# A gated stage that applies its weight and shift behind the spatial product, and a reordered last pair of attention

## The reference

```python
h = rmsnorm_2(x, norm_mix_g[i])
z = jnp.einsum('bsd,dc->bsc', h, w_in[i])
uv = jax.nn.gelu(z[..., :o1])
z_u, z_v = uv[..., :GMLP_WIDTH], uv[..., GMLP_WIDTH:]
...
a = gmlp_spatial_gating(z_u, z_v, gmlp_ln_g[i], gmlp_ln_b[i], gmlp_w_s[i], gmlp_b_s[i])
b = forgetting_attention(q, k, v, f_logit, b_f[i])
y_a = jnp.einsum('bsc,cd->bsd', a, w_branch_a[i])
y_b = jnp.einsum('bsc,cd->bsd', b, w_branch_b[i])
merged = gate_a * y_a + gate_b * y_b
```

```python
def gmlp_spatial_gating(z_u, z_v, ln_g, ln_b, w_s, b_s):
    v = layernorm(z_v, ln_g, ln_b)
    v = v.reshape(B, S // GMLP_BLOCK, GMLP_BLOCK, GMLP_GROUPS, GMLP_GROUP_DIM)
    ...
    w = jnp.where(mask[None], w_s, jnp.zeros_like(w_s))
    mixed = jnp.einsum('gts,bnsgc->bntgc', w, v) + b_s.T[None, None, :, :, None]
    return z_u * mixed.reshape(B, S, GMLP_WIDTH)
```

## Time and profile before

| | us |
|---|---|
| median of 3 runs | 2146.32 |
| lowest and highest of them | 2143.61 to 2148.26 |
| profiled execution | 2146.56 |
| its span, first to last instruction | 2144.5 |
| TensorE busy in it | 2093.4 |
| VectorE busy in it | 1319.3 |
| ScalarE busy in it | 876.8 |
| GpSimd busy in it | 345.2 |

### The profile page before, as it was taken

One profiled execution on the slowest core, in us unless ns is written; L12 is line 12 of the kernel. 1 busy time (PEld: TensorE's weight loads), 2 busy tenths in 40 slices (PEclk: granted clock), 3 DMA queues, 4 the chain that ended last, 5 costly groups with the idle time before them and its releaser, 6 DMA issues.

```text
span 2144.5 us, 28580 instructions
## 1 busy us (share of the span) xinstructions
PE 2093.4 (98%) x9448; PEld 1719.8 (80%) x9448; DVE 1319.3 (62%) x1597; ACT 876.8 (41%) x1257; POOL 345.2 (16%) x254
## 2 busy tenths in 40 slices
PE   7999999999999999999999999989999999999998
PEld 4888888788878878888887788867888888888876
DVE  5877578668744553333357877767333577547767
ACT  5322223377533342222245656653222344334444
POOL 2999998000000200000000000021000000000000
PEclk8999999899999989999999999999999999999999
DMA  8665664322233323233323222232433233333222
GB/s 290 185 186 174 199 189 141 100 69 68 69 89 103 104 71 97 84 100 98 90 80 104 70 69 68 69 74 65 118 96 92 86 98 90 88 106 98 74 83 88
DMA packets 372868, 226.33 MB, mean 106 GB/s; under 512 B 8481, under 2 KB 361922, under 8 KB 372816
## 3 DMA queue, kind: packets, MB, share of 16 engines
q1 hardware_dynamic: 362976, 193.49, 30.9%
q0 software_dynamic: 9840, 32.16, 5.5%
HBM read 223.52 MB, written 2.10 MB: 105 GB/s over the span
## 4 chain that ended last, share of the span: by engine, by line
PE 90%; DVE 5%; ACT 2%; issue 1%; DMA 1%; SPq 1%; POOL 0%; DVEq 0%; ACTq 0%
PE ps L486 28%; PE ps L487 28%; PE ps L488 28%; PE ps L610 1%; PE ps L598 1%; DVE wl L1437 1%; PE ps L599 1%; PE ps L625 1%; PE ps L626 1%; DVE inv L1461 0%; PE ps L830 0%; DMA xtok<-in_x 0%; DMA wada<-in_w_ada 0%; SPq L384 0%; PE ps L601 0%
## 5 line engine op out<-in xcount | busy, mean ns | idle before, releaser
L486 PE MATMUL ps<-uh,wh 128*128 128x512 f32 x1848 | 729.6, 395 | 12.5 <-DVE ul L1489 5.5
L487 PE MATMUL ps<-ul,wh 128*128 128x512 f32 x1848 | 723.8, 392 | 0.0
L488 PE MATMUL ps<-uh,wl 128*128 128x512 f32 x1848 | 723.3, 391 | 0.0
L1437 DVE TENSOR_TENSOR wl<-raw,wh 128x1024 fp32r<-128x1024 f32 x389 | 562.7, 1451 | 205.1 <-ACT wh L963 198.9
L963 ACT ACTIVATE wh<-raw 128x1024 fp32r<-128x1024 f32 x389 | 407.6, 1052 | 190.3 <-PE ps L488 187.7
L486 PEld LDWEIGHTS ps<-uh,wh 128*128 128x128 f32 x1848 | 349.6, 189 | 85.9 <-issue 13.7
L488 PEld LDWEIGHTS ps<-uh,wl 128*128 128x128 f32 x1848 | 349.6, 189 | 73.8
L487 PEld LDWEIGHTS ps<-ul,wh 128*128 128x128 f32 x1848 | 349.7, 189 | 71.6 <-issue 0.5
L486 PE MATMUL ps<-ah,wh 128*128 128x512 f32 x528 | 208.9, 396 | 0.0
L487 PE MATMUL ps<-al,wh 128*128 128x512 f32 x528 | 208.8, 396 | 0.0
L488 PE MATMUL ps<-ah,wl 128*128 128x512 f32 x528 | 208.8, 395 | 0.0
(11 more groups left out here) (318 smaller groups left out, 2389.4 us busy)
## 6 DMA issues: line engine op xcount, KB each, us to landing
raw<-in_ffn_w_gu SPq DMA_DIRECT2D x88, 512.0 KB, 4.5
raw<-in_w_in SPq DMA_DIRECT2D x57, 512.0 KB, 3.8
ada_ring<-in_w_ada POOLq DMA_DIRECT2D x56, 512.0 KB, 4.1
raw<-in_w_up SPq DMA_DIRECT2D x44, 512.0 KB, 3.8
raw<-in_w_mix_in SPq DMA_DIRECT2D x40, 512.0 KB, 3.9
raw<-in_ffn_w_down SPq DMA_DIRECT2D x32, 384.0 KB, 3.2
raw<-in_ffn_w_down SPq DMA_DIRECT2D x32, 320.0 KB, 3.0
wada<-in_w_ada SPq DMA_DIRECT2D x16, 512.0 KB, 9.8
```

The costliest lines, as they stand in the source:

```text
L486: pe.matmul(dst, lh, rh, start=first, stop=False, skip_group_check=True)
L487: pe.matmul(dst, lh, rl, start=False, stop=False, skip_group_check=True)
L488: return pe.matmul(dst, ll, rh, start=False, stop=last, skip_group_check=True)
L1437: dve.tensor_tensor(wl[:, w], raw[:, w], wh[:, w].bitcast(F32), ALU.subtract).then_inc(w_lo, 1)
```

## The change

Weight and shift of the layer normalisation move behind the mixing. Since w_s mixes positions and the weight is per channel, W(v*g + b) is g*(W v) + W b. DVE no longer multiplies by ln_g and adds ln_b per group. TensorE mixes the bare normalised values and makes W b in three more matmuls of 128x128 per group, into bank 6 or 7. DVE adds that to b_s in a 128x128 tile, and its bias instruction becomes a multiply by a column of ln_g and an add. POOL splits ln_b into high and low parts (a cast and a subtraction per group), and loads three tiles per group in place of four; ln_g comes with the vectors loaded at the start.

The order of the last pair changes. TensorE runs `z_in(0)` and `z_in(1)` before the first head's values, `z_in(2)` and the first `turn_w` before the second head's, and group 0 is normalised before the second head's output is summed. Group 0's tiles are loaded and masked during the first pair. In the group loop z m+3 stands behind mix m for every m up to 4. z is drained into a tile of its own, `gz`, not into halves of `tmp`. The first branch chunk waits for its input tile by tile.

```diff
+Z_BANK = (B_O, 0, 1, 0, 1, 0, 1, 0)
@@ TensorE, attention body
                     if last:
+                        if kind == 2:
+                            pe.wait_ge(A_["o_s"], 2 * p + 1)
                         next_first()
...
-                    if last and kind == 1:
+                    if last:
                         next_middle()
+                    if last and kind == 2:
+                        pe.wait_ge(A_["t_lo"], 6 * p + 3)
+                        turn_forget()
+                        pe.wait_ge(G["z"], 3)
                     values(t, A_, p, 0)
@@ TensorE, merge
+                    dense(nb + 2, 0, 2, kt, xa[0], xa[1], ready=ready_a)
...
+                    dense(nb + 3, 0, 3, kt, xb[0], xb[1])
@@ TensorE, gated stage
+            def third_z():
+                z_in(2)
+                pe.wait_ge(A["att2"]["t_lo"], 6 * 8)
+                turn_w(0)
-            attention("att2", t2, 2, 8, 3, lambda: z_in(0), None, lambda: z_in(1))
+            attention("att2", t2, 2, 8, 3, lambda: z_in(0), lambda: z_in(1), third_z)
...
                     mm = mm3(bank(2 + s % 2, b * P, P), gvh[:, v], gvl[:, v], gwh[:, w], gwl[:, w], True, True)
+                pe.wait_ge(G["b_lo"], m + 1)
+                mm = mm3(bank(6 + s % 2, 0, P), gsr[s][:, 3 * P:4 * P], gsr[s][:, P:2 * P], gwh[:, w], gwl[:, w], True, True)
                 mm.then_inc(G["mix"], 1)
-            z_in(2)
-            turn_w(0)
-            z_in(3)
             for m in range(DT):
                 if m + 1 < DT:
                     turn_w(m + 1)
                 mix_group(m // 4, m % 4)
-                if 1 <= m < 5:
+                if m + 3 < DT:
                     z_in(m + 3)
-                elif 5 <= m < 7:
+                elif m < 7:
                     merge_gate("merge2", 0, m - 5)
@@ ACT
+            def z_out(m):
+                done(AT_["zu"] + m, 0)
+                act.activation(tile(gz, m), bank(Z_BANK[m]), ACT.Gelu_apprx_tanh).then_inc(G["z"], 1)
...
             for m in range(DT):
-                act.wait_ge(G["w_tr"], m + 1)
-                act.activation(gwh[:, (m % 2) * P:(m % 2 + 1) * P], bank(4 + m % 2, 0, P), ACT.Copy).then_inc(G["w_hi"], 1)
-                act.wait_ge(G["n3"], m + 1)
-                act.wait_ge(G["mix"], m + 1)
-                act.activation(gvh[:, :], sq[:, 0:S], ACT.Copy).then_inc(G["v_hi"], 1)
+                if m > 0:
+                    weight_hi(m)
+                    group_hi(m)
                 if m + 2 < DT:
                     split(nb + m + 2 + LEAD, 0)
                 act.wait_ge(G["a"], m + 3)
                 act.activation(tile(gah, m), sq[:, S:2 * S], ACT.Copy).then_inc(G["a_hi"], 1)
-                if m + 2 < DT:
-                    z_out(m + 2)
+                if m + 3 < DT:
+                    z_out(m + 3)
@@ DVE, last pair
+                    if last and kind == 2:
+                        stream_slice(p)
+                        split(AT_["zu"] + LEAD, 0)
+                        f_rows(p)
                     o_sum(p, 0)
-                    if kind == 2:
+                    if kind == 2 and not last:
                         f_rows(p)
+                    if last and kind == 2:
+                        layer_stats()
                     turned_lo(p, 1)
...
+                    elif kind == 2:
+                        split(AT_["zu"] + 1 + LEAD, 0)
+                        first_group()
                     o_sum(p, 1)
@@ DVE, group
-                dve.tensor_tensor(v4, v4, ln_g.unsqueeze(1).to_broadcast([P, ST, P]), ALU.mult).then_inc(G["n2"], 1)
-                dve.tensor_tensor(v4, v4, ln_b.unsqueeze(1).to_broadcast([P, ST, P]), ALU.add).then_inc(G["n3"], 1)
...
+                bf = gsm[s][:, 2 * P:3 * P]
+                dve.tensor_tensor(bf, bank(6 + s % 2, 0, P), bf, ALU.add).then_inc(G["bf"], 1)
...
+                dve.scalar_tensor_tensor(ssq[:, :].rearrange("p (b c) -> p b c", b=ST), bank(2 + s % 2).rearrange("p (b c) -> p b c", b=ST),
+                                         cols[:, C_LNG + m:C_LNG + m + 1], bf.unsqueeze(1).to_broadcast([P, ST, P]),
+                                         ALU.mult, ALU.add).then_inc(G["bs"], 1)
@@ POOL
+            def mask_group(m):
+                pool.wait_ge(G[f"ld{m % 4}"], 48 * (m // 4 + 1))
+                pool.tensor_tensor(gsm[m % 4][:, 0:P], gsm[m % 4][:, 0:P], gmask[:, :], ALU.mult).then_inc(G["mask"], 1)
+                hi = gsr[m % 4][:, 3 * P:4 * P]
+                pool.tensor_copy(hi, gsm[m % 4][:, P:2 * P]).then_inc(G["b_hi"], 1)
+                pool.wait_ge(G["b_hi"], m + 1)
+                pool.tensor_tensor(gsr[m % 4][:, P:2 * P], gsm[m % 4][:, P:2 * P], hi.bitcast(F32), ALU.subtract).then_inc(G["b_lo"], 1)
```

More of the change, by code:

```diff
@@ L215, in build @@
         ncum = place("ncum", [64, S], F32R, late)
-        gah = place("gah", [P, DT * S], F32R, rows(14))
-        gal = place("gal", [P, DT * S], F32R, rows(22))
+        gah = place("gah", [P, DT * S], F32R, rows(22))
+        gal = place("gal", [P, DT * S], F32R, rows(14))
+        gz = place("gz", [P, DT * S], F32, rows(14))
         gvh = place("gvh", [P, S], F32R, rows(8))
@@ L221, in build @@
         gwl = place("gwl", [P, 2 * P], F32R, rows(10) + 1024)
-        gsm = [place(f"gsm{x}", [P, 4 * P], F32, at) for x, at in enumerate((rows(11), rows(12), late, late + row))]
+        gsm_at = (late + row, rows(11), rows(12), late)
+        gsm = [place(f"gsm{x}", [P, 4 * P], F32, at) for x, at in enumerate(gsm_at)]
+        gsr = [place(f"gsr{x}", [P, 4 * P], F32R, at) for x, at in enumerate(gsm_at)]
         ptok = place("ptok", [P, ST * 256], F32, rows(0))
@@ L656, in first_scores, with turn_forget @@
                         turn_values()
+                def turn_forget():
+                    for j in range(ST):
+                        mm = pe.transpose(bank(B_FT, j * P, P), tmp[:, j * P:(j + 1) * P], ident[:, :])
+                    mm.then_inc(A_["f_tr"], 1)
                 def body(p, last, first=False):
@@ L1179, in body @@
                     if last and kind == 2:
[L1180 to L1181 removed]
+                        for b in range(ST):
+                            gelu_rows(b)
+                        split(AT_["zu"] + LEAD, 0)
+                        z_out(1)
+                        act.wait_ge(A_["f_tok"], 1 + pairs)
+                        v = vtok[:, :].rearrange("p (b n) -> p b n", b=ST)[:, :, (pairs - 1) * P:pairs * P]
+                        act.activation(v, v, ACT.Gelu_apprx_tanh).then_inc(G["vg"], 1)
                     if kind == 1:
@@ L1590, in ffn, with normal_group, weight_lo, group_lo @@
                                     scaled_lo(2 * i + r, *lift)
+            def normal_group(m):
+                dve.wait_ge(G["v_lo"], m + 1)
+                for b in range(ST):
+                    x = dve.tensor_scalar(sq[:, b * P:(b + 1) * P], vtok[:, b * D + m * P:b * D + (m + 1) * P], bnmv[:, 2 * b:2 * b + 1],
+                                          rstd[:, b:b + 1], ALU.subtract, ALU.mult)
+                x.then_inc(G["n1"], 1)
+            def weight_lo(m):
+                dve.wait_ge(G["w_hi"], m + 1)
+                w = slice((m % 2) * P, (m % 2 + 1) * P)
+                dve.tensor_tensor(gwl[:, w], bank(4 + m % 2, 0, P), gwh[:, w].bitcast(F32), ALU.subtract).then_inc(G["w_lo"], 1)
+            def group_lo(m):
+                dve.wait_ge(G["v_hi"], m + 1)
+                dve.tensor_tensor(gvl[:, :], sq[:, 0:S], gvh[:, :].bitcast(F32), ALU.subtract).then_inc(G["v_lo"], 1)
+            def first_group():
+                dve.wait_ge(G["sd"], 1)
+                dve.reciprocal(rstd[:, :], rstd[:, :]).then_inc(G["sd"], 1)
+                dve.wait_ge(G["sd"], 2)
+                normal_group(0)
+                weight_lo(0)
+                group_lo(0)
             def attention(name, t, kind, pairs):
@@ L2052, in group @@
-            def group(m):
-                i, s = m // 4, m % 4
-                dve.wait_ge(G["w_hi"], m + 1)
-                w = slice((s % 2) * P, (s % 2 + 1) * P)
-                dve.tensor_tensor(gwl[:, w], bank(4 + s % 2, 0, P), gwh[:, w].bitcast(F32), ALU.subtract).then_inc(G["w_lo"], 1)
-                dve.wait_ge(G["v_hi"], m + 1)
-                dve.tensor_tensor(gvl[:, :], v_, gvh[:, :].bitcast(F32), ALU.subtract).then_inc(G["v_lo"], 1)
+            nb = AT_["zu"]
+            def group(m):
+                s = m % 4
+                if m > 0:
+                    weight_lo(m)
+                    group_lo(m)
```

135 lines of the change are left out of this document (61 added, 74 removed).

## The result

The changed kernel takes 2159.01 us (median; 2157.83 to 2160.46), against 2146.36 for the kernel before: 1.0059 times as long, interval 1.0043 to 1.0075. It is slower, as forecast, but by 12.7 us where 7.0 were forecast, and 1.0 us above the range's end.

What follows compares the result with a forecast made beforehand. TensorE was taken to bound the kernel, with its matmuls, idles and half-clock stretches. Terms -8.0, +6.0, +0.5 and +8.5 of clock gave +7.0 on 2146.56, so 2153.3 us for a median; range 2145 to 2158.

Steps and rivals of the forecast that it cites:

- The mechanism: Mix 1 to mix 5: ACT's drain waits for z m+3, holding gwh and gvh, so TensorE stalls; 11.25 us in all.
- The term: TensorE's wait after each z chunk for drain, gwh, gvh and gvl: 2.25 us, for mix 1 to mix 5.
- The last pair: First z chunk to mix 0: the ACT and DVE chain sets mix 0, 28.2 us after z 0, -8.0 us.
- the clock's term: Low TensorE clock after six new idles: five of six at 1.7 us, +8.5; bounds none and 13.8.
- Rival 1: Low clock after all six new idles at the dearer price: +12.3 us, 2158.6 us; chance 0.13.
- The rest of the sum: Mix 0 to branch a without clock: periods, last mix, bias matmuls and five stalls, 63.5 us, +6.0.
- The branches: First two branch chunks: 11.31 us before, +0.5 as ACT and DVE come late to the second's weight chunk.
- The two idles that were to go: Mix 0 to branch a: idle of 4.42 goes as turn_w 2 follows z 3, 2.90 as the branch waits tile-wise.
- Rival 3: Group loop: ACT reaches gvh in time, so stalls and most clock loss vanish; -12.75 us, 2133.6 us; chance 0.12.
- Rival 4: POOL's 16 new instructions each lengthen a DVE instruction on the chain by 0.22 us: 3.5 us more, 2156.8; chance 0.05.
- The saving on DVE: Multiply and add dropped for 8 groups, some 11 us busy time, costed at nothing since DVE waits for ACT.

Runs made afterwards that it cites:

- The moved drain: Changed kernel with ACT's drain of z m+2 right behind gvh of m, replacing z m+3's drain ahead of gwh: 2137.6 us, 0.9962 times the kernel before.
- the fill: Changed kernel with 11 matmuls that nobody reads behind each of z 3 to z 7, filling the stalls: 2146.6 us, 1.000 times the kernel before.
- putting the statistics back: Changed kernel with the statistics behind a_ptl on DVE, as before the change: 2158.0 us in one execution.
- a filled gap: Kernel with the drain moved behind gvh, plus 14 matmuls that nobody reads behind z 2, ahead of turn_w 0: 2135.95 us, 0.9948 times the kernel before.
- the kernel with the masks ahead: Drain moved, last pair reordered on ACT and DVE, seven unread matmuls behind z 2, POOL's masks ahead of waiting loads: 2134.0 us, 0.9950 times the kernel before.
- the one with less work on DVE: Kernel before, without DVE's multiply by ln_g and addition of ln_b, nothing in their place: 2139.95 us, 0.9973 times the kernel before.

## Why the prediction went wrong

**The mechanism was right.** Each of five drains held `gwh` and `gvh` behind a whole z chunk, and TensorE stood for it. The term was 2.25 us a stall. From the last matmul of z 3 at 1438.10 plus a pitch of 0.23 to mix 1 at 1440.64 it is 2.3, with the short `turn_w` in it. The moved drain took stalls and clock away together, the fill took the clock away alone.

**The last pair was right.** 27.96 against 28.2, and 3.62 us of idle ahead of `turn_w` 0 against some 4. Nor did errors cancel: DVE begins the statistics 17.46 us after z 0 (17.62 in the prediction's sum) and `a_ptl` 22.53 after it (22.70). That the idle lies inside the chain and costs nothing by itself was shown by putting the statistics back: no change of mix 0.

**The failed step is the size of the clock's term.** The prediction took five of six low stretches at 1.7 us, 8.5. All six came, at 1.7 to 3.4, 16.6: 8.1 too little. The count was off by one. The price was the greater error: 1.7 had been taken from the idle nearest in length, for every stall alike, and the stretches behind mix 1, 3 and 5 were low over some 7 us. The 1.7 was no misreading: 6 us from 1412.14 in the kernel before have a clock of 0.72, which is 1.7 too. What failed is the step from one idle's price to another idle of like length. The rows had shown that price can differ (2.0 and 2.6), and the prediction put these into a rival, whose upper end of 13.8 was still short of 16.6; why 3.4 follows some of these idles stays open. Rival 1 is what happened in kind, dearer than priced. That its 2158.6 lies so near the measured 2159.0 is in part luck: it had +12.3 for the stretch, and the stretch lost 14.5.

**The rest of the sum** from mix 0 to branch a, without the clock: 79.42 - 16.6 = 62.8 against 63.5. The branches came out at +0.8 against +0.5; TensorE waits 0.64 for the second branch's low part. The two idles that were to go (4.42 and 2.90) went. The -2.9 ahead of z 0 hid part of the miss in this profile: the stretch alone lost 14.5 where 7.0 were forecast.

**Rival 3** (the drain does not hold the product) was wrong as to the kernel, and too high as to its worth: with the drain elsewhere the stretch took 7.3 us less than before, where that rival had 12.75. The low stretch behind mix 0 and the idles of 0.2 to 0.3, some 4 us, make most of the difference.

**Rival 4** (POOL beside DVE) had a row and no effect on the time. POOL's mask, which stood beside four `gvl` before (0.91 to 0.92 us), stands beside four of the eight `gal` now, which take 0.86 where the other four take 0.69:

```profile
1435.41 0.86 DVE L2125 TENSOR_TENSOR gal<-sq,gah 128x512 fp32r<-128x512 f32 x1 [0.70 <-ACT gah L1422]
```

```profile
1435.93 0.66 POOL L2296 TENSOR_TENSOR gsm<-gsm,gmask 128x128 f32<-128x128 f32 x1
```

The trace lists nothing that waited for these `gal`. The rule that the prediction drew from the Trainium skill, "GPSIMD Engine Reference", section "1. Specifications", that GpSimd and VectorE contend when VectorE reads two SBUF inputs, agrees in kind with these times; they cost nothing here.

**The saving on DVE** was put at nothing for this order, and DVE stood 3.06 us ahead of `gwl` in the first of these periods. By itself, in the order of before, it was worth 1.9 us of the stretch.

## What to carry to other kernels

When an instruction that drains one product is moved, look at which chunk it now drains and what stands behind it on its engine: here one index (m+3 in place of m+2) in the same place made the drain wait for work that TensorE had only just begun. Put what the next product needs ahead of a drain that waits. Price an idle of TensorE at itself plus the low clock behind it, take at least the dearest price that the trace shows, which was still too low here (2.6 against 3.4), and test it with matmuls that nobody reads: they part the two.

## What the runs showed of the hardware

The same idle had different sequels. An idle of 2.03 us was followed by 1.7 or by 3.4 us lost at half clock; one of 2.08, behind a filled gap, by none; one of 1.39, in the kernel with the masks ahead, by 1.7. The idle of 2.90 ahead of branch a left the clock at 1.00 in the kernel before and at 0.72 over 6 us in the one with less work on DVE. Five idles of 0.97 in a row left it at 1.00. The runs show that the length of the idle alone does not tell what follows; what does was not settled.
